# First weight quarter ahead of x, x in two column halves, zero products for TensorE, and the third chunk rounded ahead of the statistics

## The reference

```python
def reference(x, positions, ...):
    x = first_block(x, ...)     # 2 layers: rms_norm, 4 token mixers, merge, rms_norm, SwiGLU
    return second_block(x, ...) # 2 layers: the same plan; the last feed-forward has 8 experts, top 2
...
def rms_norm(x, g):
    y = xf * lax.rsqrt(jnp.mean(xf * xf, axis=-1, keepdims=True) + NORM_EPS)
    return (y * g.astype(jnp.float32)).astype(x.dtype)
...
def mixer_block(h, ...):
    u = h @ w_in                # 1024 x 8220: queries, keys, values, gates of four mixers
```

## Time and profile before

| | us |
|---|---|
| median of 3 executions | 2505.57 (2505.15 to 2506.05) |
| the profiled execution | 2506.58 |
| its span, first to last instruction | 2504.9 |
| matmuls busy in it | 2482.8 (99%) |
| VectorE, ScalarE, POOL busy | 1814.3 (72%), 1520.2 (61%), 152.7 (6%) |
| first matmul of any kind starts at | 6.98 |
| first wide product starts at | 10.80 |

### The profile page before, as it was taken

The page is one execution under the profiler, slowest core; times in us unless marked ns, Lnnn a source line. Parts: engine busy times, 40 slices in busy tenths (PEclk is TensorE's granted clock), DMA queues, the critical chain, the costliest instruction groups (busy, mean ns, idle before and its releaser), DMA issues.

```text
span 2504.9 us, 31923 instructions
## 1 busy us (share of the span) xinstructions
PE 2482.8 (99%) x11820; PEld 2044.6 (82%) x11820; DVE 1814.3 (72%) x1839; ACT 1520.2 (61%) x1581; POOL 152.7 (6%) x133
## 2 busy tenths in 40 slices
PE   8999999999999999999999999999999999999998
PEld 7888888888888888888888887888888888888877
DVE  6687655657775555665446567989989899898988
ACT  6565544555554455555446556777777777777776
POOL 0102000020020000110000023000000000000010
PEclk9999999999999999999999999999999999999999
DMA  7444555544455564555555456999999999999996
GB/s 261 151 162 171 174 186 191 173 156 151 168 177 190 186 211 157 173 181 185 184 185 168 168 179 241 382 369 386 381 380 385 375 384 376 385 371 388 367 409 252
DMA packets 90682, 633.75 MB, mean 253 GB/s; under 512 B 10461, under 2 KB 10837, under 8 KB 15840
## 3 DMA queue, kind: packets, MB, share of 16 engines
q1 hardware_dynamic: 85584, 616.63, 66.7%
q0 software_dynamic: 4720, 15.57, 1.7%
q10 hardware_dynamic: 288, 0.33, 0.0%
HBM read 625.00 MB, written 7.48 MB: 252 GB/s over the span
## 4 chain that ended last, share of the span: by engine, by line
PE 98%; DMA 1%; DVE 0%; issue 0%; ACT 0%; SPq 0%; ACTq 0%; DVEq 0%
PE bank L785 14%; PE bank L787 13%; PE bank L786 13%; PE bank L1363 8%; PE bank L1365 8%; PE bank L1364 8%; PE bank L1336 4%; PE bank L1338 4%; PE bank L1337 4%; PE bank L767 4%; PE bank L800 4%; PE bank L802 4%; PE bank L801 4%; PE bank L1188 1%; PE bank L1190 1%; PE bank L1189 1%
## 5 line engine op out<-in xcount | busy, mean ns | idle before, releaser
L1906 DVE TENSOR_TENSOR w_lo<-raw,w_hi 128x2048 fp32r<-128x2048 f32 x583 | 1341.8, 2304 | 413.4 <-ACT w_hi L1453 400.7
L1453 ACT ACTIVATE w_hi<-raw 128x2048 fp32r<-128x2048 f32 (+1 forms) x588 | 1120.1, 1906 | 259.7 <-PE bank L802 117.3
L785 PE MATMUL bank<-w_hi,xhi 128*128 128x512 f32 x1456 | 578.9, 398 | 1.0 <-DVE w_lo L1916 0.4
L787 PE MATMUL bank<-w_lo,xhi 128*128 128x512 f32 x1456 | 567.8, 390 | 0.0
L786 PE MATMUL bank<-w_hi,xlo 128*128 128x512 f32 x1456 | 567.3, 390 | 0.0
L1363 PE MATMUL bank<-w_hi,xhi 128*128 128x512 f32 x896 | 358.7, 400 | 0.8 <-issue 0.4
L1365 PE MATMUL bank<-w_lo,xhi 128*128 128x512 f32 x896 | 350.0, 391 | 0.0
L1364 PE MATMUL bank<-w_hi,xlo 128*128 128x512 f32 x896 | 349.6, 390 | 0.0
L785 PEld LDWEIGHTS bank<-w_hi,xhi 128*128 128x128 f32 x1456 | 273.5, 188 | 63.0 <-issue 4.8
L787 PEld LDWEIGHTS bank<-w_lo,xhi 128*128 128x128 f32 x1456 | 273.3, 188 | 58.3
L786 PEld LDWEIGHTS bank<-w_hi,xlo 128*128 128x128 f32 x1456 | 273.8, 188 | 53.3
(11 more groups left out here) (382 smaller groups left out, 2365.0 us busy)
## 6 DMA issues: line engine op xcount, KB each, us to landing
raw<-in_wexpert SPq DMA_DIRECT2D x336, 1024.0 KB, 4.9
raw<-in_wdense SPq DMA_DIRECT2D x248, 1024.0 KB, 4.8
expert_rows<-y POOLq DMA_DIRECT2D x7, 512.0 KB, 4.8
expert_rows<-back POOLq DMA_DIRECT2D x3, 512.0 KB, 3.9
x<-in_x SPq DMA_DIRECT2D x2, 512.0 KB, 4.7
raw<-in_wdense SPq DMA_DIRECT2D x4, 256.0 KB, 6.1
biasT<-bias_rows POOLq DMA_DIRECT2D x1, 1024.0 KB, 6.9
normal_rows<-hnorm POOLq DMA_DIRECT2D x1, 1024.0 KB, 7.7
```

Of the source, the lines that this page charges most:

```text
L785: mm(bank[banks[t]][:, :], xhi[:, k0 + k, tok], wh, start=start and k == 0, stop=False)
L787: last = mm(bank[banks[t]][:, :], xhi[:, k0 + k, tok], wl, start=False, stop=stop and k == 3)
L1453: return nc.scalar.activation(dst, src, f, **kw)
L1906: V.tensor_tensor(lo[:, c % RAW, :], raw[:, c % RAW, :], hi[:, c % HI, :].bitcast(F32), ALU.subtract).then_inc(lo_ready, 1)
```

## The change

It does five things.

1. SP requests piece 0 of chunk 0 first, then columns 0 to 511 of x for all tokens (`x_first`), piece 1, columns 512 to 1023 of x (`x_loaded`), and pieces 2 and 3. It was x by tokens, then all pieces.
2. ScalarE and VectorE round and split piece 0 before they wait for the parameters.
3. TensorE transposes only tiles 0 and 1 (the first column half) ahead of chunk 0. Tiles 2 and 3 are transposed in the middle of chunk 0, as part of `rest_of_norm`.
4. VectorE sets a 128 x 512 tile to zero first. TensorE makes three products of it at the start and one between the transposes and chunk 0, into bank X[3], which nobody reads before it is overwritten.
5. ScalarE runs `conv(2)` directly behind `conv(1)`, ahead of `Exp` and `statistics()`, and not at position 0 of the mixer.

```diff
+            def fetch_piece(i):
+                w = slice(512 * i, 512 * i + 512)
+                sp.dma_start(raw[:, 0, w], a["wdense"][0][:, w]).then_inc(first_in[i] if i < 3 else raw_full[0], 16)
+            def fetch_columns(o, arrived):
+                sp.dma_start(x[:, :, o:o + 512], a["x"][0][:, o:o + 512].rearrange("(t p) d -> p t d", p=P)).then_inc(arrived, 16)
             def fetch_first():
-                for i in range(4):
-                    w = slice(512 * i, 512 * i + 512)
-                    sp.dma_start(raw[:, 0, w], a["wdense"][0][:, w]).then_inc(first_in[i] if i < 3 else raw_full[0], 16)
+                fetch_piece(0)
+                fetch_columns(0, x_first)
+                fetch_piece(1)
+                fetch_columns(512, x_loaded)
+                for i in (2, 3):
+                    fetch_piece(i)
...
-            for t in range(NT):
-                sp.dma_start(x[:, t, :], a["x"][0, t * P:t * P + P, :]).then_inc(x_loaded, 16)
...
-                        pe.wait_ge(x_loaded, 16 * NT)
+                        pe.wait_ge(x_first if i < 2 else x_loaded, 16)
...
-                if READY[key] is not None:
-                    norm(key, (2, 3))
+                norm(key, (2, 3))
...
+            def zero_products(n):
+                for i in range(n):
+                    mm(bank[X[3]][:, :], gates[:, 0, 0:P], gates[:, 0, 0:512], start=True, stop=True)
+            pe.wait_ge(warm_set, 1)
+            zero_products(3)
             pe.wait_ge(ident_loaded, 16)
...
-                    if ready is None or k[2] == "moe":
+                    if ready is None:
+                        norm(k, (0, 1))
+                        zero_products(1)
+                    elif k[2] == "moe":
                         norm(k, range(4))
...
                 if n == 0:
+                    conv_first(0)
                     act.wait_ge(par_loaded, 16)
...
-                        for piece in ((0,), (1, 2, 3))[i]:
+                        for piece in ((1,), (2, 3))[i]:
                             conv_first(piece)
                 if n == 0:
                     round_narrow(0)
                     conv(1)
+                    conv(2)
...
-                    if pos > 0 or k == phases[1]:
+                    if pos > 0:
                         conv(c0 + pos_step(k, pos) + 2)
...
+            V.memset(gates[:, 0, 0:512], 0.0).then_inc(warm_set, 1)
```

More of the change, by code:

```diff
@@ L426, in program @@
         up_done = sem("branch_half_done")
+        warm_set, x_first = sem("warm_tile_set"), sem("x_first_columns_in")
         x_loaded, cst_loaded, par_loaded = sem("x_loaded"), sem("cst_loaded"), sem("par_loaded")
@@ L1485, in squares @@
                     if n == 0:
-                        act.wait_ge(x_loaded, 16 * NT)
+                        act.wait_ge(x_first, 16)
+                        act.wait_ge(x_loaded, 16)
                     for b, v in ready or []:
@@ L2714, in load @@
                 pool.dma_start(dst, src).then_inc(par2_loaded, 16)
-            pool.wait_ge(x_loaded, 16 * NT)
+            pool.wait_ge(x_first, 16)
+            pool.wait_ge(x_loaded, 16)
             pool.dma_start(onehot[:, :], a["onehot"]).then_inc(bias_loaded, 16)
```

## The result

The change made the kernel slower by a little. The median over 20 executions is 2509.19 us, against 2505.54 us for the kernel before over 20: +3.65 us, a ratio of 1.0014 with a 95% interval of 1.0007 to 1.0020. That is within 0.2%. It lies outside the forecast range, 2505.2 to 2508.6, and is nearly twice the +1.9 us forecast. One execution at 3170 us, with a granted clock of 0.735, is left out of the ratio (without it the median is 2509.17); the others lie between 2506.94 and 2510.69.

The account below looks back on a forecast made before the run. TensorE, busy 2482.8 of 2504.9 us, was taken as the bound, with everything decided in the opening. The `z_lo` delay of 1.9 us, the head's -0.1 not added, on the median 2505.57 gave 2507.4; range 2505.2 to 2508.6.

Parts of the forecast that it names:

- the view's "issue": Wait of 0.4 us before the products on `zs`, read as `z_lo`; rival that `z_lo` did not hold them: 2506.9, 10%.
- The early head: TensorE's opening: narrow products could start 0.55 us earlier, but the wait for `cst` leaves 0.1; rival that it comes through: 2505.0.
- the narrow products: TensorE after chunk 0: could start at 15.9 us but wait for `cst` until about 16.35.
- 1.9 (`z_lo`): Chunk 2's wait on ScalarE delays VectorE's split of chunk 3, so `z_lo` and the product on it come 1.9 us later.
- The estimate of 18.8: Landing time in us of chunk 2's transfer, for which ScalarE would wait from 16.3.
- The two 0.4 us of opposite sign: POOL's requests sliding behind `cst`, up to 0.4 us earlier; x in 2 KB rows, up to 0.4 us slower; taken as 0.
- Covered, by 0.5 us: Chunk 1 is split by 18.7 us, and TensorE wants it at 19.2, behind the narrow products.
- Head: -0.1 us: Edits 1 to 4 in the opening: 0.55 us won before the narrow products, only 0.1 left after the wait for `cst`.
- The clock falls: Rival: new TensorE idle stretches at `cst`, `narT` and `z_lo` lower the clock, 5.1 us more, 2512.6 in all; 4%.
- the deadlines: Points where TensorE needs another engine's result: `cst` before the narrow products, then `narT`, then `z_lo`; they absorb an earlier head.

Follow-up runs that it names:

- the z operations ahead: VectorE does its z operations of position 2 ahead of the split of chunk 4: 2507.97 us on the whole change, 2505.31 us on the kernel before.
- the fillings of `narT` and `zs`: Whole change with its routing filled, plus five unread products ahead of the wait for `narT`: 2505.58 us; plus four ahead of the wait for `z_lo`: 2505.71 us.
- the routing is filled: 18 products that nobody reads placed ahead of three TensorE waits in the experts' routing: 2503.14 us on the kernel before, 2506.14 us on the whole change.
- the last version: Kernel before with routing filled, z operations ahead, three zero products at the start and the wait for `cst` one position later: 2501.81 us.

## Why the prediction was wrong

**Right:** the kind and place of the loss. ScalarE stands at the transfer of chunk 2, `narT` becomes a new wait (forecast 26.85, seen 27.09), `z_lo` holds the products on `zs` (forecast 46.5, seen 46.88), and the view's "issue" there was indeed `z_lo`, as moving the z operations ahead showed on both kernels. The early head is worth nothing, and the zero products cost nothing and gain nothing at the end.

**Right by luck: the narrow products.** They came at 16.44, forecast 16.3 to 16.5. But the forecast had chunk 0 done at 15.6 and TensorE waiting for `cst`. In fact the wide products began 0.7 us late and chunk 0 ended at 16.4, with `cst` there at 5.93 + 10.3 = 16.2: TensorE did not wait for it in this execution. (With the same head it waited 0.28 us in the profile of the z operations ahead, where the narrow products came at 17.00.)

**Wrong, the sum.** It had one term, 1.9, and took everything else as equal in both kernels. The measured +3.65 consists of:

| | us | where it is seen |
|---|---|---|
| `z_lo` | 2.24 | the mark on `zs`; 2.0 to 2.4 over the six traces in which TensorE waited there |
| outside the span | 0.2 | time less span, 1.8 against 1.6; 1.8 to 1.9 in all experiments with edits 1 to 3, and 1.6 in all without |
| the clock in the opening | 0.4 to 0.6 | the fillings of `narT` and `zs` |
| the rest | 0.6 to 0.8 | not shown; see "Left open" |

The prediction took its difference from the trace and added it to the median, so the time outside the span was taken as equal. Why these edits lengthen it is not known; the zero products are not the cause, as it is 1.8 without them.

**The term that was too small: "1.9 (`z_lo`)".** It measured 2.24. 0.3 of it is the landing of chunk 2. The estimate of 18.8 was itself a little off: two steps of 2.5 us back from 23.7 are 18.7. The two 0.4 us of opposite sign were taken as 0; the request (timeline) and its time to landing (DMA view) of the changed kernel give 6.45 + 12.6 = 19.1 and not 18.8:

```profile
6.45 0.43 SPq L733 DMA_DIRECT2D raw<-in_wdense  x1
...
raw<-in_wdense SPq DMA_DIRECT2D x1, 1024.0 KB, 12.6
```

With the old order of requests and edit 5 alone ScalarE got it at 18.55 and 18.82 in two profiles; with the new order at 18.9 to 19.5 in eight that waited for it. What in the new order makes it later was not separated. It is not the later request alone: without zero products chunk 2 was requested at 6.68 and was there by 19.1 all the same. What would fit is that POOL's requests now slide in between `cst` and chunk 2: `glab`, the largest, lands at 11.7 + 6.0 = 17.7 and landed at 9.0 + 7.1 = 16.1. The chain behind chunk 2 was as long as forecast.

**Wrong, "Covered, by 0.5 us" and "Head: -0.1 us".** Edits 1 to 4 alone cost 1.4 to 2.0 us in the medians, by marks 1.4 and 1.8. The prediction checked chunk 1 only against TensorE's need for its product, at 19.2, and not against what stands behind it on ScalarE; and even there it was not covered, as TensorE began it at 19.48, some 0.25 us late. It had `x_first` landed before 6.98, since it counted bytes; it landed at 1.4 + 5.8 = 7.2. So tile 0 was copied at 8.03 and not 7.2, the wide products began at 9.9 and not 9.2, tiles 2 and 3 were copied at 13.45 and not 12.6, and chunk 1 at 15.16 and not 14.4. Even the 14.4 of the prediction was 0.7 us behind the 13.72 of before, and this should have been carried to `z_lo`. In the whole change the late chunk 1 did not show at `zs`, as ScalarE's wait for chunk 2 hid it.

**Wrong, the clock.** The rival "The clock falls" had 4% and a price of 5.1 us on top of 1.9, and the sum had nothing for it. In fact it falls in some executions for 3.4 us, at 1.7 us, and the wait at `zs` takes most of that: 0.4 to 0.6 us in the median. It was priced as all or nothing from the one fall that the trace of before shows.

**Wrong, one execution taken for all.** By the earlier trace rows the transposes alone let the clock rise, so that the zero products were worth nothing on the wide products. In all five other traces with that head the 16 transposes were slow to the last, and one to four wide products behind them too. In the change without zero products the head was 2.3 us slower. That it made no difference to the result is due to the deadlines, as forecast, and not to that reading.

**Left open.** 3.65 less 3.00 is 0.65 us that disappear when the routing is filled; taken against the kernels before beside each it is 3.65 less 3.39, 0.26. The filling wins 2.8 us on the kernel before and 3.05 on the changed one. The changed kernel reaches the routing 2.3 us later (1529.09 against 1526.83 for the first router product); that a later arrival meets the slow clock worse more often would fit, but the nine unfilled traces do not show it: the routing takes 16.3 and 15.0 us in the two that come early and 13.5 to 16.2 in the seven that come late. Medians of the kernel before differ by 0.5 us between batches, on the same chip too (2505.95 and 2505.47), so all of it may be chance.

## What to carry to other kernels

An operation that only waits for a transfer must not be moved ahead of work that others need: on an engine with a fixed order it turns slack of its own into lateness for everything behind it. Check a moved step against what stands behind it on its own engine, and not only against the consumer of its result. Where TensorE is the bound, an early start is worth something only after the deadlines behind it have been moved, each found as the wait that the stream just meets; here these were `cst` and `z_lo`. And where short waits of TensorE cannot be avoided, a few products that nobody reads in their place may be worth more than the waits themselves. Last, one trace is one execution: here the head, the routing and the opening each had a slow and a quick form, and a margin of half a microsecond read from one trace was none.

## What the runs showed of the hardware

The clock of TensorE fell to the lower level, 1.2 GHz, behind idle stretches of 0.6, 0.9 and 1.4 us (by the view of waits, at `narT`) within an otherwise dense stream, for some 3.4 us. It did so in three of the five traces that have this stretch (edit 5 alone, with and without the filled routing, and the z operations ahead) and not in the whole change, where it was 1.1 us both times. In the 13 traces without it the clock did not fall there. Nor did it fall behind the idle stretch at `zs`, which was 0.7 to 1.5 us long in six traces. So in the opening the fall came only behind an idle stretch, but its length does not tell when. The Trainium skill, "TensorE: Matmul & The Clock Gate", "Why this matters for your kernels", warns there of longer gaps; the trace of edit 5 alone does not bear out that shorter ones are safe, with 0.52 in the window from 29 to 32 us.

How long it stays low at the start varies as much. With the head of the kernel before, the pace doubled 3.0 us after the first transpose in one trace and 4.6 to 5.6 us after it in five; in the run without zero products the eight transposes and nine wide products from 7.32 to about 14.4 us were all slow. Zero operands too bring the clock up: the six halves of the three zero products took 5.49 us in four executions, 5.15 in that of the changed kernel and 4.46 in that of the last version, that is, the pace rose while they ran, and the transposes behind them were fast for the most part (with the new head 8 in 1.06 to 1.29 us, against 1.94 for the 8 without zero products). The windows print a granted clock of 1.00 from the start on, also where the pace is the slow one, so at the start of a span the pace is the evidence.
